# A narrow score group of latent attention moved one round forward, between the steps of two scans

## The reference, cut to what matters

```python
for li in range(2):
    y_att  = _mla(c_q, c_kv, k_pe, ...)      # 4 heads, 1040 tokens
    y_rwkv = _rwkv_bidir(u, v_first, ...)    # scan forwards and scan backwards
# inside _mla, for a block of queries
s = einsum('bqhd,bkhd->bhqk', qn, k_nope) + einsum('bqhd,bkd->bhqk', qp, k_pe)
p = softmax(s * scale, axis=-1)
o = einsum('bhqk,bkhd->bqhd', p, v)
```

## Time and profile before

| what | us |
|---|---|
| median of 3 runs | 5523.99 |
| lowest and highest run | 5523.89, 5526.87 |
| span of the profiled execution | 5519.8 |
| TensorE matmul busy | 4898.7 |
| VectorE busy | 3334.8 |

### The profile page before, as it was taken

One profiled execution on the slowest core, in us unless ns is written; L12 is line 12 of the kernel. 1 busy time (PEld: TensorE's weight loads), 2 busy tenths in 40 slices (PEclk: granted clock), 3 DMA queues, 4 the chain that ended last, 5 costly groups with the idle time before them and its releaser, 6 DMA issues. The chain is left out here.

```text
span 5519.8 us, 128974 instructions
## 1 busy us (share of the span) xinstructions
PE 4898.7 (89%) x56564; PEld 4170.6 (76%) x56564; DVE 3334.8 (60%) x5051; ACT 2133.5 (39%) x3885; POOL 1683.3 (30%) x1036
## 2 busy tenths in 40 slices
PE   6989999998799956989999998799966998999999
PEld 5888888886577746878888886577755766788887
DVE  5435655558688864345655557688865455563552
ACT  2323333332277752333333332177753234232331
POOL 0013322222277740012332222177741100022221
PEclk9999999998799987989999998799987998999999
DMA  4410101013366653410101004266653101233333
GB/s 131 140 50 19 31 19 29 20 29 110 104 227 229 233 182 101 133 52 18 31 20 30 19 18 118 93 226 229 227 182 121 35 5 54 88 97 121 111 92 111
DMA packets 383085, 536.30 MB, mean 97 GB/s; under 512 B 136482, under 2 KB 306594, under 8 KB 354466
## 3 DMA queue, kind: packets, MB, share of 16 engines
q1 hardware_dynamic: 339714, 488.61, 27.8%
q0 software_dynamic: 41472, 34.21, 2.1%
q10 hardware_dynamic: 1344, 5.24, 0.3%
HBM read 573.01 MB, written 122.09 MB: 126 GB/s over the span
## 5 line engine op out<-in xcount | busy, mean ns | idle before, releaser
L267 PE MATMUL ps<-w,xbT 128*128 128x512 f32 x2304 | 570.6, 405 | 89.5 <-DVE w L2399 89.5
L2399 DVE TENSOR_TENSOR w<-w,w 128x2048 fp32r<-128x2048 f32 x192 | 545.5, 2868 | 75.2 <-ACT w L2356 75.2
L267 PEld LDWEIGHTS ps<-w,xbT 128*128 128x128 f32 x2304 | 439.3, 194 | 193.0 <-DVE w L2399 101.4
L267 PE MATMUL ps<-hT,w_in 128*128 128x416 f32 (+1 forms) x2736 | 490.9, 338 | 9.0 <-DVE w_in L748 9.0
L267 PEld LDWEIGHTS ps<-hT,w_in 128*128 128x128 f32 x2736 | 457.7, 195 | 34.9 <-issue 28.9
L1473 POOL TENSOR_TENSOR lm<-Ab,consts 116x416 f32<-116x416 f32 x240 | 254.5, 1068 | 611.7 <-PE ps L267 334.8
L2356 ACT ACTIVATE w<-w 128x2048 fp32r<-128x2048 f32 x192 | 362.6, 1937 | 97.5 <-DMA w<-in_moe_w_dram,widx 97.5
L267 PE MATMUL ps<-v,pT 104*104 104x128 f32 (+1 forms) x2176 | 274.2, 283 | 28.2 <-issue 27.4
L267 PE MATMUL ps<-w,actT 128*128 128x512 f32 x1152 | 278.4, 390 | 5.8 <-POOL w L2348 3.0
L267 PEld LDWEIGHTS ps<-v,pT 104*104 104x104 f32 (+1 forms) x2176 | 252.8, 181 | 40.0 <-issue 32.3
L2348 POOL TENSOR_TENSOR w<-w,w 128x1024 fp32r<-128x1024 f32 x96 | 268.6, 2798 | 29.1 <-ACT w L2392 27.6
(11 more groups left out here) (445 smaller groups left out, 11222.9 us busy)
## 6 DMA issues: line engine op xcount, KB each, us to landing
w<-in_moe_w_dram SPq DMA_DIRECT2D x192, 1024.0 KB, 8.2
w_gate<-in_w_gate_dram SPq DMA_DIRECT2D x44, 512.0 KB, 3.8
w_up<-in_w_up_dram SPq DMA_DIRECT2D x44, 512.0 KB, 3.8
w_down<-in_w_down_dram SPq DMA_DIRECT2D x44, 512.0 KB, 3.2
w_in<-in_w_in_dram SPq DMA_DIRECT2D x36, 512.0 KB, 4.4
ys<-t_ys SPq DMA_DIRECT2D x20, 832.0 KB
t_h<-x SPq DMA_DIRECT2D x30, 416.0 KB
w_out<-in_w_out_dram SPq DMA_DIRECT2D x24, 512.0 KB, 7.6
```

Of the source, the lines that this page charges most:

```text
L267: made = e.matmul(out, a, b, start=start, stop=stop)
L2399: e.tensor_tensor(w.lo, w.x, w.hf, ALU.subtract).then_inc(*P.c("moe_dve").tick(li, "w13", b, k))
```

## The change

All three score groups of an item are issued at k = 0. Nothing is issued at k = 1 on TensorE. The loop now stands inside the branch `if k == 0`. The instructions, their operands and their semaphores are the same; five matmuls per item move ahead of the scan phases that stood between the two rounds. The lists of the other engines are not touched.

```diff
@@ -1561,8 +1561,7 @@
                 if h == 0:
                     e.wait_ge(*P.d("att_kpe_in").at(li))
             e.wait_ge(*P.d(f"att_q{s}_in").at(li, item))
-        if k < 2:
-            for g, (t0, tn) in list(enumerate(GROUPS))[2 * k:2 * k + 2]:
+            for g, (t0, tn) in enumerate(GROUPS):
                 if item:
                     e.wait_ge(*(ac if g == 2 else dv).at(li, "pT", item - 1, g))
                 out, ts = P.ps[4 + g][0:C, 0:tn], slice(t0, t0 + tn)
```

## The result

| what | before | after |
|---|---|---|
| median of 5 runs, us | 5523.89 | 5551.02 |
| lowest to highest, us | 5521.15 to 5526.87 | 5547.24 to 5551.44 |
| span of the profiled execution, us | 5519.8 | 5547.5 |
| ratio of the times | | 1.0047, 95% interval 1.0034 to 1.0059 |

The change costs 27 us, 0.47%, where 19 were forecast. The device time of the profiled execution after is 5549.52 us, so 2.0 us lie around its span. The 4.2 us that the prediction carried on compared a median with the span of another execution: some 2 of them were scatter.

What follows compares the result with a forecast made beforehand. TensorE was taken to bound the recurrence, where lost microseconds count fully. Terms of 9.5 us per layer, 19.0 for two, took the span from 5519.8 to 5538.8; plus 4.2 gave 5543.0 us, range 5531 to 5556.

Steps and rivals of the forecast that it cites:

- The 4.2 us: Difference between the median and the profiled span before the change, added to the forecast span to give a forecast median.
- Slower, because cover is taken away: Main forecast: moving the narrow score group uncovers scan round trips on TensorE, 19.0 us slower; chance 0.68.
- Place 13, +0.56: Items starting at round 13: nothing left between TT,XX and the next T,lm; 3.36 against 2.80 us, +0.56 each.
- Places 8 and 20, +0.20 each: Items starting at rounds 8 and 20: only rh,TT covers the copy XX; 2.39 against 2.19 us, +0.20 each.
- Place 2, -0.13: Items starting at round 2: one entry into a score group saved on TensorE; 1.61 against 1.74 us, -0.13 each.
- Entering is paid once: Leaving a scan group for a score group costs 0.13 us; merged groups pay it once, the narrow one staying 0.83.
- The edges, +0.65 each: A layer's first and last items, beside one scan direction only: 2.39 against 1.74 us, +0.65 each.
- VectorE's shorter wait is worth nothing: VectorE's maxima wait less for scores (152.7 us in 124 cases before), but this was costed at nothing.
- The sum: All place and edge terms added: 9.5 us per layer, 19.0 for two layers.
- No hole opens: At place 2, two kr,hb products of the other direction still stand between T,lm and its reader.
- The clock rival: Added holes drop the granted clock from 2.4 to 1.2 GHz after each: 49 us, 5592; chance 0.02.

Runs made afterwards that it cites:

- only13: Kernel before, with all three score groups at k = 0 only for items starting at place 13; median 5539.65 us, ratio 1.0023.
- not13: Kernel before, with all three score groups at k = 0 for items starting at places 2, 8 and 20; median 5534.85 us, ratio 1.0015.
- only8_20: Kernel before, with all three score groups at k = 0 only for items starting at places 8 and 20; median 5546.78 us, ratio 1.0038.
- wide_late: Kernel before, with first wide and narrow groups at k = 0, second wide group at k = 1, query load waiting for it; 5533.27 us, ratio 1.0013.
- base: Kernel before, unchanged, measured and profiled a second time; median 5525.62 us, ratio 0.9995.
- dve13: Kernel before, with VectorE's backward hb and kr at place 13 held until after the forward T and TT additions; 5532.72 us, ratio 1.0015.
- after_dve13: Changed kernel, with VectorE's backward hb and kr at place 13 held until after the forward additions; 5567.35 us, ratio 1.0084 against the kernel before.

## Why the prediction was right or wrong

- *Slower, because cover is taken away.* Right. The sign, the mechanism and the places are shown by the steps of `only13`, `not13`, `only8_20` and `wide_late`.
- *Place 13, +0.56.* Right: 0.83 for the group ahead, 0.85 more behind `TT,XX`, 1.12 less for the group and its wait make +0.56, and 1.72 was measured in each of six steps. `only13` has 0.58. The reason given, a backlog that ends just before it matters, is shown by the two distances of 12.70 and 13.26.
- *Places 8 and 20, +0.20 each.* Undersized: 0.24 each. At place 20 `T,lm` to `XX,TT` is 1.60, since `T,lm` behind a score group takes 0.81 and not the 0.78 that I took from a row behind a wait; at place 8 the distance is 1.55, but the group that restarts after the wait takes 0.04 more.
- *Place 2, -0.13.* Oversized. Entering a score group costs 0.10, not 0.13 (`T,lm` 0.91 before, 0.81 after), and half of the saving is lost at once, since `kr,hb` of phase 13, now earlier, waits for VectorE's `Ab`. What is left is 0.04 to 0.05. "No hole opens" was true, but the place was not free of VectorE.
- *Entering is paid once.* Right for the merged group: 0.83 at all four places. The rule of the Trainium skill (TensorE: Matmul & The Clock Gate, Step-by-step: what each phase is for) by which weight loads are pulled ahead does not make entering free here: it is 0.10.
- *The edges, +0.65 each.* At the last item `T,lm` to its reader is 1.60 in place of the 1.56 forecast. With the 0.83 ahead that is +0.69 at either edge. They are 2.6 us of the sum, and no run takes them alone.
- *VectorE's shorter wait is worth nothing.* Right: 64 us less of it, and no step that is shorter by it.
- *The sum.* 19.0 forecast. The forecast step grew by 0.83 (-0.13 + 0.20 + 0.20 + 0.56), the measured by 1.02. With the measured terms in place of the forecast ones the same sum gives about 11.2 a layer, 22.5 for both: the errors at places 2, 8 and 20 and at the edges are small, but all go the same way. The medians say 27 and 22. In the first pair of profiles the recurrences together grew by 22.3 us; the 3 of the clock are in that, while the sixth step of the first recurrence did not grow and some steps before were up to 0.6 us over 86.5. What goes beyond 22.5 is, as far as is known, the 3 us of the clock and scatter: the stretch between the recurrences was 7 us shorter in the first profile of the kernel before than in `base`. The prediction had put the clock at nothing.
- *The clock rival.* It was dismissed because the clock is 1.00 beside holes of 0.6 to 0.8 us. That holds from the second step of a recurrence on: there it stayed at 1.00 with the new holes as well, in both profiles of the changed kernel. In the first step it does not hold, and the earlier trace rows are from a first step: the clock had fallen to 0.50 at 400 to 402 us, just ahead of them, after a stretch (396 to 398) in which TensorE was busy 0.98 of 2.00 us. The rival's price of 49 us, for a fall after each of 60 holes, is far off; one fall of 6 us behind the first item of the second recurrence, about 3 us, is what the profiles of the changed kernel show.

## What to carry to other kernels

A total of busy time or of waits does not say whether an order matters: read what stands between a group and the group that needs its result, and compare its length with the uncovered round trip. A filler placed a few rows earlier is no filler. A hole on the busiest engine is only worth what the next engine's chain leaves of it: ask, before closing one, when the instructions that follow would be released by the others. Where a scan has only one direction to work on, holes add up, and the granted clock of that stretch belongs among the rows to read.

## What the runs showed that I had not expected

- The round trips are constant to a few hundredths: 1.55 to 1.60 us TensorE, ScalarE, TensorE; 1.72 us with VectorE's two additions, in each of the six middle steps of `after`, `only13`, `dve13` and `after_dve13`.
- Near 60% busy, VectorE is a bound in rounds 13 to 16 of each step: a mere swap of two of its operations with two others, all the same work, made the step 0.66 us longer.
- Executions of one kernel spread by 27 us. Two profiles of the kernel before differ by 6.7 us in the first step of the first recurrence, by how long the granted clock falls back from 1.00 to 0.50 after it has first risen.
